# A hybrid attention encoder on one core: a key remainder, two projections, four values and a root moved by a step, and turns of the identity added at the start

## The reference

```python
u = _rmsnorm(h, g_mix[l]);  z = u @ w_in[l]
c_q  = _rmsnorm(z[..., OFF_CQ:OFF_CKV], g_q[l])       # 256 latent columns
c_kv = _rmsnorm(z[..., OFF_CKV:OFF_KR], g_kv[l])      # 256
k_rope = _rope(z[..., OFF_KR:OFF_DQ], cos, sin)       # 32, shared by the 8 latent heads
q = c_q @ w_uq[l]     # 8 heads: 64 plain + 32 rotated
kv = c_kv @ w_ukv[l]  # 8 heads: 64 key + 64 value
o_mla = softmax(q k^T * scale) v                      # k = [kv key, k_rope]
# 4 differential heads, two maps each, with a distance bias
w = softmax(q0 k0^T + bias) - lam * softmax(q1 k1^T + bias)
o_diff = _rmsnorm(w @ dv, g_sub[l]) * (1 - lam_init)
h = h + concat(o_mla, o_diff) @ w_out[l]
h = h + square(relu(_rmsnorm(h, g_mlp[l]) @ w_up[l])) @ w_down[l]
```

## Time and profile before

| | us |
|---|---|
| median of 3 runs (lowest, highest) | 1208.68 (1206.12, 1209.07) |
| the profiled execution | 1210.87 |
| its span, first to last instruction | 1209.0 |
| PE busy in it | 1189.2 |
| DVE, ACT, POOL busy | 882.8, 600.4, 582.3 |
| mean granted clock of TensorE | 0.993 of 2.4 GHz |

### The profile page before, as it was taken

How to read it: one execution, slowest core, us unless ns; L and a number is a source line. 1 busy time by engine, 2 the same in 40 slices (tenths; PEclk the granted TensorE clock), 3 DMA queues, 4 the chain that set the end, 5 groups by cost and what they waited for, 6 DMA issues and landing times.

```text
span 1209.0 us, 16359 instructions
## 1 busy us (share of the span) xinstructions
PE 1189.2 (98%) x5672; PEld 974.2 (81%) x5672; DVE 882.8 (73%) x1356; ACT 600.4 (50%) x986; POOL 582.3 (48%) x371
## 2 busy tenths in 40 slices
PE   8999999999999999999999999999999999999997
PEld 7887678888888888888887776888888888888886
DVE  4657867656779776889856677776658778767896
ACT  5345766743544344435423466666444544344443
POOL 1014554622865676565510145537047665766462
PEclk8999999999999999999999999999999999999999
DMA  5521110134234322431324201102342334223402
GB/s 160 157 70 62 45 24 30 53 87 147 76 92 139 106 90 87 137 105 36 105 58 121 70 27 44 36 18 88 86 159 89 87 105 140 88 81 111 140 13 92
DMA packets 128132, 104.56 MB, mean 86 GB/s; under 512 B 5514, under 2 KB 107956, under 8 KB 128052
## 3 DMA queue, kind: packets, MB, share of 16 engines
q1 hardware_dynamic: 127840, 103.50, 28.9%
q10 hardware_dynamic: 84, 0.02, 0.0%
q0 software_dynamic: 128, 0.00, 0.0%
HBM read 99.84 MB, written 2.10 MB: 84 GB/s over the span
## 4 chain that ended last, share of the span: by engine, by line
PE 93%; DVE 2%; POOL 2%; DMA 1%; ACT 1%; issue 1%; SPq 0%; POOLq 0%; DVEq 0%; ACTq 0%
PE bank L1520 82%; PE bank L1590 3%; PE bank L1618 3%; PE bank L1561 2%; DMA stage<-in_w_in 1%; POOL rs L621 1%; PE bank L1538 1%; DMA xin<-in_x 1%; DVE k_pack L1177 0%; PE bank L1698 0%; PE bank L1690 0%; PE bank L1547 0%; PE bank L1753 0%; DVE w_lo L1066 0%; POOL e_x L630 0%
## 5 line engine op out<-in xcount | busy, mean ns | idle before, releaser
L1520 PE MATMUL bank<-u_hi,w_hi 128*128 128x512 f32 x760 | 299.3, 394 | 0.3
L1520 PE MATMUL bank<-u_hi,w_lo 128*128 128x512 f32 x760 | 296.1, 390 | 0.0
L1520 PE MATMUL bank<-u_lo,w_hi 128*128 128x512 f32 x760 | 295.9, 389 | 0.0
L750 ACT ACTIVATE w_hi<-stage 128x1024 fp32r<-128x1024 f32 (+2 forms) x141 | 136.4, 977 | 225.8 <-DMA stage<-in_w_up 92.2
L1066 DVE TENSOR_TENSOR w_lo<-stage,w_hi 128x1024 fp32r<-128x1024 f32 (+2 forms) x116 | 136.6, 1187 | 57.6 <-ACT w_hi L750 57.2
L1520 PEld LDWEIGHTS bank<-u_hi,w_hi 128*128 128x128 f32 x760 | 142.8, 188 | 31.0 <-issue 2.5
L1520 PEld LDWEIGHTS bank<-u_hi,w_lo 128*128 128x128 f32 x760 | 142.7, 188 | 30.3
L1520 PEld LDWEIGHTS bank<-u_lo,w_hi 128*128 128x128 f32 x760 | 142.9, 188 | 28.3
L750 ACT ACTIVATE w_hi<-b 128x1024 fp32r<-128x1024 f32 x84 | 89.0, 1059 | 129.8 <-PE bank L1520 88.8
L1520 PE MATMUL bank<-w_hi,quad_hi 128*128 128x512 f32 x392 | 152.6, 389 | 0.0
L1520 PE MATMUL bank<-w_hi,quad_lo 128*128 128x512 f32 x392 | 152.5, 389 | 0.0
(11 more groups left out here) (237 smaller groups left out, 2293.6 us busy)
## 6 DMA issues: line engine op xcount, KB each, us to landing
stage<-in_w_up SPq DMA_DIRECT2D x64, 512.0 KB, 4.1
b<-in_w_down SPq DMA_DIRECT2D x56, 512.0 KB, 3.5
stage<-in_w_in SPq DMA_DIRECT2D x32, 512.0 KB, 3.9
stage<-in_w_out SPq DMA_DIRECT2D x16, 512.0 KB, 3.6
stage<-in_w_down SPq DMA_DIRECT2D x8, 512.0 KB, 3.4
xin<-in_x SPq DMA_DIRECT2D x4, 512.0 KB, 7.1
stage<-in_w_ukv SPq DMA_DIRECT2D x4, 512.0 KB, 3.5
out<-yout SPq DMA_DIRECT2D x8, 256.0 KB, 2.4
```

The lines of the kernel that those rows point to most:

```text
L750: last = nc.scalar.activation(hi(w_hi, s)[:, :, d:d + n], st(r)[:, :, f:f + n], ACT.Copy)
L1520: mm = nc.tensor.matmul(acc, a, b, start=first and t == 0 and m == 0, stop=last and t == len(terms) - 1 and m == 2)
```

## The change

Four edits. (1) In the table of projections, q2 goes from step 17 to 16, kp1 from step 19 to 18 (it is now listed by hand), v3 from step 16 to 19. (2) The last differential head's root: POOL takes it a step later, in step 21, behind the scaling of tile 20; PE turns it into a row in step 21 still, but behind turn 20 instead of ahead of it. (3) The rotated key's copy on ACT goes from step 12 to 11, its remainder on DVE from step 13 to 12. (4) PE makes 12 more turns of the identity behind the turn of the gains, and 5 more between the second and the third turn of the input.

```diff
@@ -77,11 +77,11 @@
             n += 2
 
 
-    for use, n in (("v0", 8), ("v1", 9), ("kp0", 10), ("q0", 11), ("v2", 12), ("q1", 14), ("v3", 16), ("q2", 17)):
+    for use, n in (("v0", 8), ("v1", 9), ("kp0", 10), ("q0", 11), ("v2", 12), ("q1", 14), ("q2", 16), ("kp1", 18), ("v3", 19)):
         fill[n].append((use, range(KC)))
     for hd in range(MLA_HEADS - 2):
         n = DSTEPS + 1 + TT * hd
-        if hd % 2 == 0:
+        if hd % 2 == 0 and hd:
             fill[n + 2].append((f"kp{hd // 2 + 1}", range(KC)))
         if hd:
             fill[n + hd % 2].append((f"q{hd + 2}", range(KC)))
@@ -709,7 +709,7 @@
                     else:
                         normalise(l, n - 1 - DSTEPS)
                     g, r = divmod(n - 8, TT)
-                    if r == 0 and 0 <= g < DIFF_HEADS:
+                    if (r == 0 and 0 <= g < DIFF_HEADS - 1) or (r == 1 and g == DIFF_HEADS - 1):
                         power(l, MISC_AT[f"sub{g}_c"], 3 + g, rs)
                     for use in ended(n - 2):
                         if use[0] == "q":
@@ -931,7 +931,7 @@
                     g, r = divmod(n - 7, TT)
                     if r == 0 and 0 <= g < DIFF_HEADS + MLA_HEADS:
                         pv_out(l, g)
-                    if n == DSTEPS - 4:
+                    if n == DSTEPS - 5:
                         act.wait_ge(kr_ready, val(kr_ready, l, 2))
                         act.wait_ge(sc_done, val(sc_done, l, 2 * (DSTEPS - TT)))
                         nc.scalar.activation(k_pack[NOPE:P, 0, 0, :], krf[NOPE:P, :], ACT.Copy).then_inc(krb_hi_made, 1)
@@ -1351,7 +1351,7 @@
                     g, r = divmod(n - 8, TT)
                     if r == 0 and DIFF_HEADS <= g < DIFF_HEADS + MLA_HEADS - 1:
                         pv_out(l, g)
-                    if n == DSTEPS - 3:
+                    if n == DSTEPS - 4:
                         dve.wait_ge(krb_hi_made, val(krb_hi_made, l, 1))
                         nc.vector.tensor_tensor(k_pack[NOPE:P, 0, 1, :], krf[NOPE:P, :],
                                                 k_pack[NOPE:P, 0, 0, :].bitcast(F32), ALU.subtract
@@ -1675,10 +1675,15 @@
 
 
             pe.wait_ge(consts_made, 4)
-            for i in range(16):
-                nc.tensor.transpose(bank[7][:, 0:P], ident[:, :], ident[:, :])
+            def keep_busy(count):
+
+                for i in range(count):
+                    nc.tensor.transpose(bank[7][:, 0:P], ident[:, :], ident[:, :])
+
+            keep_busy(16)
             pe.wait_ge(gm_in, 16)
             nc.tensor.transpose(bank[1][:, 0:G_MLP], g_rows[0:G_MLP, :], ident[0:G_MLP, 0:G_MLP]).then_inc(gt_done, 1)
+            keep_busy(12)
 
             def first_turn(j):
 
@@ -1697,7 +1702,10 @@
                     for m, w in enumerate(wtile(SLOT[0], k)):
                         nc.tensor.matmul(bank[BANK["cq0"]][:, :], w, u_hi[:, k, :], start=(k == 0 and m == 0), stop=False)
 
-            for j in range(4):
+            for j in range(2):
+                first_turn(j)
+            keep_busy(5)
+            for j in range(2, 4):
                 first_turn(j)
             pe.wait_ge(gt_copied, 1)
             pe.wait_ge(gm_in, 16)
@@ -1809,7 +1817,7 @@
                         score_pair(l, n + 1)
                     if r == 2 and 0 <= g < DIFF_HEADS:
                         stat_c(l, MISC_AT[f"sub{g}_c"], tmp_s[:, 1, :])
-                    if r == 3 and 0 <= g < DIFF_HEADS:
+                    if r == 3 and 0 <= g < DIFF_HEADS - 1:
                         stat_b(l, MISC_AT[f"sub{g}_b"], 3 + g)
                     if r == 3 and g >= DIFF_HEADS:
                         half_values(l, g + 1, 0)
@@ -1819,6 +1827,8 @@
                         values(l, g)
                     if n:
                         turn(l, n - 1)
+                    if r == 3 and g == DIFF_HEADS - 1:
+                        stat_b(l, MISC_AT[f"sub{g}_b"], 3 + g)
                     if n + 2 == DSTEPS:
                         scores(l, n + 2)
```

## The result

| | before | changed |
|---|---|---|
| median of 6 runs each, us | 1207.97 | 1214.63 |
| lowest, highest | 1206.12, 1210.37 | 1213.33, 1216.19 |
| the profiled execution, its span | 1210.87, 1209.0 | 1215.02, 1213.2 |

The ratio is 1.0055 (95% interval 1.0039 to 1.007): 6.7 us slower, where 3.7 were predicted.

A forecast was written before the change was run, and what follows sets the result against it. TensorE's own stream, 93% of the chain, was taken as the bound. Terms -3.1 + 0.7 + 4.6 = +2.2 us, with one half-clock stretch of 1.65 us +3.8, applied to the median 1208.68, gave 1212.4 us; range 1206.0 to 1216.5.

The forecast's parts named there:

- The clock and the start (-3.1): At the input: added identity turns fill PE's idle gaps at no cost and keep 2.4 GHz; -3.1 us.
- the prediction's other bound: At the start: added turns at 0.217 us each end at 7.9 and push the input turns by 1.0 us.
- The key's remainder (+0.7): Turns 11 and 12: L1356 slowed beside POOL's subtraction, turn 12 0.33 us later; +0.7 us for two layers.
- The projections (+3.2): Steps 16 to 19: head 3's values 1.3 us later, turn 20 another 0.3 us; +3.2 us in all.
- The root (+1.2): Last differential head: the root's turns on PE follow turn 20 and 0.2 us of waiting; +0.6 us per layer.
- the whole middle: From turn 15 to head 4's values, projections and root together: values start 2.3 us later, +4.6 us for two layers.
- One more stretch at half the clock (+1.65): New waits before turn 16 and around turns 19 and 20 bring one more half-clock stretch of 1.65 us.
- That the waits go: Rival: turn 16 runs when PE is free and the waits before turn 20 go; 1203.2 us, chance 0.12.
- That the clock holds at turn 12 with smaller waits: Rival: waits at turn 12 shrink and both 1.65 us half-clock stretches go; 1207.6 us, chance 0.10.
- That it falls at every new wait: Rival: the clock drops for three or four more stretches; 1215.8 or 1217.5 us, chance 0.12.
- That the turns of the identity don't hold the clock: Rival at the start: added turns run at 0.217 us, PE goes on at 1.2 GHz; 1216.2 us, chance 0.06.

The follow-up runs named there:

- the start alone: The kernel before with only the 12 and 5 added turns of the identity; 1206.65 us against 1207.04, ratio 0.9993.
- all but the start: The changed kernel without the 12 and 5 added turns of the identity; 1213.72 us, before 1208.07 beside it, ratio 1.0058.
- the swap: The kernel before with q2 in step 16 and v3 in step 17, kp1 left in step 19; 1208.13 us against 1208.07, ratio 1.0.
- the kernel with step 17 empty: The kernel before with v3 in step 15 and q2 in step 16, kp1 left in step 19; 1212.41 us against 1207.92, ratio 1.0044.

## Why the prediction was right, and which terms were not

The side and the range (1206.0 to 1216.5) were right, and so was that the projections cost most; the forecast of 1212.4 was 2.2 us low. By its own steps:

**The clock and the start (-3.1): the failed step.** In the trace the mechanism was nearly as said: 2.94 us, full clock from 8.6 us on. That the 12 turns cost nothing was not: they held up the input's first turn by 0.3 us here and by 1.0 us in the start alone, where most of them ran at the low pace, the prediction's other bound. The size was right only against the profiled execution, and the step that failed is the last one, that the sum could be applied to the median. In 70 runs of before beside the experiments the median is 1207.8 us; 32 of them with a mean granted clock of 0.998 or more have a median of 1206.65, and the five at 0.994 or less 1210.56. The profiled one had 0.993 and 1210.87 us. Its falls at the start were a part of its distance to the median, so the median run had little of them to give back. The timed runs have no traces, so this is inferred from their mean clock and from the eight profiles without the turns, of which five had no fall there. The measured worth of the turns is 0.4 us (0.9993, 0.9981 to 1.0004), and nothing that these runs can tell in the changed kernel (1.0058 without, 1.0055 with). Had the start been put at -0.4, the sum would have been +6.5 us; measured were +6.7. That close a match is partly luck, since of the terms below the projections were put too low, the root too high and the clock's is unsettled.

**The key's remainder (+0.7).** Right: +0.33 us a layer predicted, +0.30 in the changed kernel's layer 0, the one value with no stretch at half the clock in it (the others are +0.23 to +0.33), by the way described (1.42 us for L1356, turn 11 late by 0.34, the root's input late, POOL's last subtraction 1.27).

**The projections (+3.2).** Right in mechanism, short by a fifth: +1.99 us a layer instead of 1.6. Turn 16 fixed by POOL (3.28 us behind turn 15; idle 1.26, predicted 1.5) and kp1 ahead of head 3's values (+1.24, predicted 1.3) came as said. Turn 19's wait was 1.55 us, not 1.2, and turn 20's 0.60, not 0.8. What I didn't see is DVE's 1.21 us at q2's product, hidden here and 0.7 us a layer where kp1 is not in front. kp1's new place alone explains the changed kernel up to turn 19; the empty step costs as much when it is alone, and the two don't add up.

**The root (+1.2).** The prediction's two parts, 1.6 and 0.6 us a layer, make 4.4 us; it has 4.6, from 2.3 us at head 4's values. Alone +0.45 us a layer, of the kind that was described; within the changed kernel 0.0 (19.68 against the projections' 19.65): turn 20 is 0.45 us sooner there (16.62 against 17.07 us), since the root's turns no longer stand ahead of it, and this pays for them behind it. So the whole middle is 1.97 us a layer, where 2.3 were predicted.

**One more stretch at half the clock (+1.65).** Of a right size (1.5 us at turn 20), and in the predicted places, but in the pair of profiles it can't be seen: four falls before (the long one at the start counts as two), three after. In that pair the parts are: start -2.9, of which 0.7 are lost again by 50 us in a wait for the root of the latent norms, that the start alone didn't have; turns 10 to 12 +0.6; turns 12 to 15 -2.5, where one fall of before is missing and the other lies partly in waits; turn 15 to head 4's values +3.3 and +3.4; the MLP waits and what trails them +1.6. Together 4.1 us, and the executions are 4.15 apart. Over all runs the mean clock of the kernels with waits at turns 16, 19 and 20 is lower (0.993 without the start's turns, against 0.9965 beside it), so the falls are more frequent there; which of the single waits causes a fall stays open, and so does how much of the median's 6.7 us is the clock.

**The rivals.** That the waits go is out: turns 16 and 19 wait for 1.26 and 1.55 us, though turn 20's wait is shorter (0.60 us, not 1.01), as the prediction had it. That the clock holds at turn 12 with smaller waits is out as a reason for less time: it did hold in layer 0, but the waits around the turn add to 1.97 us (0.34, 0.74, 0.89) against 1.82. That it falls at every new wait is too much: none followed turn 16, and at turns 19 and 20 there was one in three of the four layers of the changed kernel and of all but the start. That the turns of the identity don't hold the clock is out: with turns alone ahead of them, the second eight input turns took 1.09 us, the pace of the high one of the two levels (2.4 GHz). By the rule of the Trainium skill ("TensorE: Matmul & The Clock Gate", Part 4: PE-mode transpose) that transposes don't count as busy it should have been slow; the trace disagrees. The high pace is not there from the first turn, though: in the start alone it came only within the 12, with nothing but turns of the identity and the gain ahead of it on PE. The page's figure is for bf16, and no run here shows whether these float32 turns are the form that it measured.

## What to carry to other kernels

A projection's place in a TensorE-bound stream is priced by what waits beside it: two of the four steps here took 1.4 us of matmuls for nothing, and taking the work out of either cost nearly all of it elsewhere and pushed copies ahead of what a later turn needed. Before a sum from one profile is applied to a median, ask which of the profile's losses the median run has at all, above all stretches at half the clock: the mean clock of each run tells. And of two instructions that disturb each other, find the one that is waited for, and move the other past it, in the direction in which its next neighbour has time: the same key remainder cost 0.30 us a step sooner and gained 0.5 us a step later, each in the one layer without a stretch at half the clock in the way.

## What the runs showed of the hardware

- The same subtraction L1356 (64x512, both inputs in SBUF) took 0.69 us where it started 0.01 us ahead of POOL's, which then took 1.83 us instead of 1.28; started 0.28 us behind POOL's, in the other layer, it took 1.56, and POOL's was undisturbed at 1.29. In these two pairs who starts first isn't slowed, and the other pays the wait. So says the Trainium skill ("SBUF — State Buffer", Who interferes with whom), and here the traces agree.
- A fall to half the clock is not tied to a place. Behind turn 12, after a wait of 1.2 us in both layers, the swap has one in layer 0 (from 148.0 us) and none in layer 1, and the kernel with step 17 empty the other way round (from 740.7 us).
- PE's high pace does not begin at the same turn in every execution. In the three profiles without added turns that fell at the start, the input's first eight turns, from 6.5 to 6.9 us on, ran 0.11 us apart; in the other five, its first sixteen, the last of them at 9.8 us or later, ran some 0.21 us apart, while the profile's granted clock read 1.00. The pace of the instructions tells what this clock did not.
- A mean granted clock lower by 0.004 goes with some 3 to 4 us in runs of one and the same kernel (before: 1206.65 at 0.998 and more, 1210.56 at 0.994 and less), as much as the whole change was thought to be worth.
